# Expert weights fetched as 4 MB transfers instead of pairs of 2 MB ones

## The reference

```python
logits = h @ w_router + b_router;  top 4 of 32;  gate = softmax(top 4)
for each expert e, on the tokens that chose it:
    gu = xe @ w_gu[e] + b_gu[e]            # w_gu[e]: 1024 x 2048, 8 MB
    gt, up = split(gu);  gt = min(gt, 7);  up = clip(up, -7, 7)
    act = gt * sigmoid(1.702 * gt) * (up + 1)
    out = act @ w_dn[e] + b_dn[e]          # w_dn[e]: 1024 x 1024, 4 MB
y[token] += gate * out
```

## Time and profile before

| | |
|---|---|
| median of 3 runs | 1346.04 us (1345.9 to 1346.96) |
| the profiled execution | 1352.6 us, span 1350.5 us, mean granted TensorE clock 0.986 |
| PE busy | 1261.7 us, 93% of the span |
| DVE, ACT, POOL busy | 606.1, 207.5, 153.7 us |
| read from HBM | 472.06 MB, 353 GB/s over the span |
| chain that ended last | PE 74%, DMA 23%, DVE 2% |

### The profile page before, as it was taken

One profiled execution on the slowest core, in us unless ns is written; L12 is line 12 of the kernel. 1 busy time (PEld: TensorE's weight loads), 2 busy tenths in 40 slices (PEclk: granted clock), 3 DMA queues, 4 the chain that ended last, 5 costly groups with the idle time before them and its releaser, 6 DMA issues.

```text
span 1350.5 us, 18280 instructions
## 1 busy us (share of the span) xinstructions
PE 1261.7 (93%) x7708; PEld 524.7 (39%) x7708; DVE 606.1 (45%) x1013; ACT 207.5 (15%) x305; POOL 153.7 (11%) x177
## 2 busy tenths in 40 slices
PE   7999999999999989999999999999997878787885
PEld 5756766666553222233323332333322222222221
DVE  2898322311345563434434344535444444343445
ACT  4111433210311010001000000101000111000002
POOL 2110100000012120101111111102111121111000
PEclk9999999999989999999999999999999999999898
DMA  9714716464669999999999999999999999999993
GB/s 330 261 63 135 226 63 146 167 249 161 248 261 410 424 424 426 420 428 424 423 425 394 424 407 424 423 425 420 426 421 424 424 423 424 421 424 423 422 425 141
DMA packets 91229, 466.74 MB, mean 346 GB/s; under 512 B 41952, under 2 KB 44540, under 8 KB 66263
## 3 DMA queue, kind: packets, MB, share of 16 engines
q1 hardware_dynamic: 83489, 456.74, 83.3%
q0 software_dynamic: 6240, 5.37, 1.2%
q10 hardware_dynamic: 1374, 2.76, 0.6%
HBM read 472.06 MB, written 4.26 MB: 353 GB/s over the span
## 4 chain that ended last, share of the span: by engine, by line
PE 74%; DMA 23%; DVE 2%; issue 1%; SPq 0%; ACT 0%; DVEq 0%
PE PS L1757 26%; PE PS L1379 16%; PE PS L1787 14%; DMA ring<-in_w_gu 8%; DMA arena<-in_w_gu 8%; PE PS L1819 6%; DMA ring<-in_w_dn 5%; PE PS L1559 4%; DMA arena<-in_w_dn 3%; PE PS L1603 3%; PE PS L1415 2%; PE PS L1319 1%; PE PS L1646 1%; PE PS L1506 0%; DVE XX L1275 0%
## 5 line engine op out<-in xcount | busy, mean ns | idle before, releaser
L1757 PE MATMUL PS<-ring,arena 128*32 128x512 f32 x3408 | 388.8, 605 | 37.1 <-DMA ring<-in_w_gu 19.9
L1757 PEld LDWEIGHTS PS<-ring,arena 128*32 128x32 f32 x3408 | 108.4, 111 | 308.6 <-issue 300.4
L1379 PE MATMUL PS<-arena,ring 128*128 128x320 f32 x768 | 215.2, 436 | 0.1
L1787 PE MATMUL PS<-ring,arena 128*64 128x512 f32 x880 | 198.2, 600 | 14.3 <-DMA ring<-in_w_dn 14.3
L525 POOL DMA_INDIRECT arena<-h_rows,arena x120 | 129.9, 1083 | 710.6 <-DVE arena L1202 645.5
L1379 PEld LDWEIGHTS PS<-arena,ring 128*128 128x128 f32 x768 | 145.0, 191 | 59.6 <-issue 3.2
L1236 DVE TENSOR_TENSOR arena<-PS,XX 128x1024 f32<-128x1024 f32 x32 | 39.2, 1225 | 251.5 <-PE PS L1757 203.9
L795 ACT ACTIVATE arena<-arena 128x1024 f32<-128x1024 f32 x32 | 33.8, 1058 | 716.0 <-DVE arena L1241 716.0
L1757 PE MATMUL PS<-arena 128*32 128x512 f32 x1136 | 128.7, 594 | 8.6 <-DMA arena<-in_w_gu 6.5
L1787 PEld LDWEIGHTS PS<-ring,arena 128*64 128x64 f32 x880 | 62.2, 137 | 148.6 <-issue 148.5
L1172 DVE TENSOR_TENSOR XX<-PS,XX 128x1024 f32<-128x1024 f32 x32 | 39.2, 1224 | 155.5 <-PE PS L1819 155.5
(11 more groups left out here) (210 smaller groups left out, 754.3 us busy)
## 6 DMA issues: line engine op xcount, KB each, us to landing
ring<-in_w_gu SPq DMA_DIRECT2D x96, 2048.0 KB, 25.7
ring<-in_w_dn SPq DMA_DIRECT2D x46, 2048.0 KB, 24.4
arena<-in_w_gu SPq DMA_DIRECT2D x31, 2048.0 KB, 27.5
arena<-in_w_dn SPq DMA_DIRECT2D x17, 2048.0 KB, 30.4
ring<-in_w_in SPq DMA_DIRECT2D x11, 2048.0 KB, 11.1
ring<-in_w_mem_kv SPq DMA_DIRECT2D x2, 2048.0 KB, 20.9
ring<-in_cache_mem_k SPq DMA_DIRECT2D x32, 128.0 KB, 3.3
ring<-in_cache_mem_v SPq DMA_DIRECT2D x4, 1024.0 KB, 6.2
```

The source lines that it names most:

```text
L1379: last = mm(PS[:, j % 2, 0:T], w[:, k, m * P:(m + 1) * P], hT[:, k, :], start=k == 0, stop=k == KT - 1)
L1757: last = mm(PS[32 * q:32 * q + 32, 2 * i + b, :].rearrange("p (g n) -> p g n", g=2), xT[:, k, at:at + PART], w[:, :, q, :], start=k == 0, ...
L1787: last = mm(PS[64 * h:64 * h + 64, 4 + b, :], actT[:, 4 * c + j, b * BLK:(b + 1) * BLK], moe_ring(AT[(e, 4 + c)], 4)[:, j, h * 512:(h + 1) ...
```

## The change

From the chunk with turn 9 on (expert 2's first), each two neighbours in the stream, (e, 0) with (e, 1), (e, 2) with (e, 3), and (e, 4) with (e, 5), are fetched by one transfer of 4 MB, 32 KB a partition (`expert_pair`), under one semaphore. `PLACES` is turned so that the two lie in neighbouring places: turn 0 in place 7, turns 1 to 6 in places 0 to 5, turn 7 in place 6. The first eight chunks are still loaded one by one, into the places in the old order, so that each place now gets another chunk: (0, 0) goes to place 7 and is the sixth of them rather than the first. Before a pair SP waits until both places are free. PE's wait for either chunk of a pair is a wait for the whole transfer (`signalled`, `moe_loaded`, `moe_arrived`). Expert 31's two down chunks stay single. Nothing is changed in PE's, DVE's, ACT's or POOL's own instructions.

```diff
-PLACES = [(NMIX + i) % SLOTS for i in range(4)] + [SLOTS, SLOTS + 1] + [(NMIX + i) % SLOTS for i in (4, 5)]
+PLACES = [SLOTS + 1] + list(range(SLOTS)) + [SLOTS]
...
+def paired(i):
+    return i > RING and i % 2 == 1 and RINGED[i] < NCH - 2
...
+def signalled(i):
+    return PLACE[i - 1] if i and paired(i - 1) else PLACE[i]
...
 def moe_arrived(m, v):
-    s = moe_slot(m)
+    i = TURN[m]
+    s = signalled(i)
     mixer = -(-(NMIX - s) // SLOTS) if s < SLOTS else 0
-    turns = PLACE.count(s)
-    return 16 * (mixer + turns * v + PLACE[:TURN[m]].count(s) + 1)
+    own = [signalled(j) for j in range(len(RINGED)) if not (j and paired(j - 1))]
+    upto = [signalled(j) for j in range(i + 1) if not (j and paired(j - 1))]
+    return 16 * (mixer + own.count(s) * v + upto.count(s))
...
     def moe_loaded(m):
-        s = moe_slot(m)
+        s = signalled(TURN[m])
         return loaded[s] if s < SLOTS else low_in[s - SLOTS]
...
+        def expert_pair(m):
+            e, c = STREAM[m]
+            s = moe_slot(m)
+            rooms = ring[:, s:s + 2, :] if s < SLOTS else ring_low
+            if c < 4:
+                return sp.dma_start(rooms.rearrange("p s (k n) -> p (s k) n", k=2), wgu[e, :, 2 * c:2 * c + 4, :])
+            return sp.dma_start(rooms.rearrange("p s (k n) -> p (s k) n", k=4), wdn[e])
...
-        for i in range(RING):
-            m = RINGED[i]
-            if moe_slot(m) < SLOTS:
-                sp.wait_ge(*used_up[CHUNKS[NMIX - SLOTS + (i if i < 4 else i - 2)]])
+        for place in [(NMIX + i) % SLOTS for i in range(4)] + [SLOTS, SLOTS + 1] + [(NMIX + i) % SLOTS for i in (4, 5)]:
+            m = RINGED[PLACES.index(place)]
+            if place < SLOTS:
+                sp.wait_ge(*used_up[CHUNKS[next(n for n in range(NMIX - 1, -1, -1) if slot_of(n) == place)]])
...
+        def later(v, i):
+            if i and paired(i - 1):
+                return
+            m = RINGED[i]
+            if before_it(i) is not None:
+                free(v, RINGED[before_it(i)])
+            if paired(i):
+                free(v, RINGED[before_it(i + 1)])
+                expert_pair(m).then_inc(moe_loaded(m), 16)
+            else:
+                expert_chunk(m).then_inc(moe_loaded(m), 16)
+
         for i in range(RING, len(RINGED)):
-            free(0, RINGED[before_it(i)])
-            expert_chunk(RINGED[i]).then_inc(moe_loaded(RINGED[i]), 16)
+            later(0, i)
```

More of the change, by code:

```diff
@@ L439, in over_stream @@
                 bonus_part(i).then_inc(bonus_in, 16)
[L440 to L443, removed]
+            for i in range(len(RINGED)):
+                later(w, i)
             sp.wait_ge(main["dn_done"], NE * (w + 1))
```

## The result

The changed kernel takes 1349.41 us (median), before 1346.96 in the same comparison: ratio 1.0022, interval 1.0012 to 1.0032. A second build of it (E8) gave 1.0028 (1.0011 to 1.0044). By the medians it is slower by 2.5 us and the repeat by 4.5, by the ratios by 3.0 and 3.8; 4.2 were forecast.

A forecast was written before the change was run, and what follows sets the result against it. Bound: transfers up to 558 us, PE to 789, transfers to 1300.22, then PE and DVE. Late starts +7.0, larger pieces -1.0 and -3.5, clock +1.7 make +4.2: 1350.2 us, range 1348.7 to 1352.5.

The forecast's parts named there:

- First late start: Expert 5's down product near 558 us: (5, 4) now waits for (5, 5), +3.5 us kept until 789.
- fall of the clock: TensorE dropping to 1.2 GHz after longer waits: 1.7 us at each exposed place, one expected, bounds 0 and 3.4.
- The early stream: Transfers up to 558 us: larger pieces save 1.0 us over 15 pairs.
- the later first pair: Turns 9 and 10 now wait for both places, some 7 us later; taken as 0, between 0 and 2 us.
- The stream behind 789 us: Transfers from 789 to 1300 us: larger pieces save 3.5 us over 50 pairs.
- the forecast's fit: Main queue's 2 KB and 16 KB rates give 0.0373 ns a byte plus 8.2 ns a piece.
- rival 3: Both sides cancel: no clock fall on the path, 11 ns a piece; +1.1 us, 1347.1 us; chance 0.25.
- Second late start: Expert 31's gate-up near 1300 us: (31, 0) now waits for (31, 1), +3.5 us.
- The final transfers are not late for that: At the end: expert 31's down product begins only when DVE lets it, at 1326.21, so no added delay.
- Gathers: POOL's small pieces share engines with longer ones; landing of 8.0 us may near 16, cost taken as 0.
- Rival 1: Transfers clearly faster if a transfer's end or start costs the stream: 0.2 us a pair, 1341.7 us; chance 0.12.
- rival 2: Large pieces give nothing, only late starts and a clock fall remain: +8.7 us, 1354.7 us; chance 0.15.

The follow-up runs named there:

- E8: The full change built and run a second time, against the kernel before: 1351.61 us, ratio 1.0028.
- E1: Kernel before with its 2 MB transfers; only PE's wait widened to both chunks of a pair before starting the first: 1353.25 us, ratio 1.0041.
- E3: Changed kernel, but the pairs (31, 0) with (31, 1), (31, 2) with (31, 3), (30, 4) with (30, 5) stay 2 MB transfers: 1349.66 us, ratio 1.001.
- E6: Changed kernel with places reordered so three of four pairs aren't neighbours: still 4 MB transfers, those in 16 KB pieces: 1352.76 us, ratio 1.005.
- E5: Changed kernel, but only pairs from (7, 0) up to expert 27's down pair are 4 MB, chunks at both edges single: 1343.34 us, ratio 0.9972.
- E7: Kernel before, but each 2 MB chunk is fetched by two 1 MB transfers in 8 KB pieces, PE waiting for both: 1361.78 us, ratio 1.0102.
- E2: Changed kernel, but expert 5's two down chunks stay two 2 MB transfers: 1347.59 us, ratio 1.0002.
- E4: Changed kernel with expert 5's down chunks and the last three pairs all kept as single 2 MB transfers: 1345.74 us, ratio 0.9998.

## Why the prediction was right

The sign, the size (forecast 1350.2, measured 1349.41 us) and the mechanism held: two late starts, a faster stream that does not quite pay for them, and PE's regime in between that keeps what it gets. That the two times are only 0.8 us apart is partly luck: the growth was 2.5 to 3.0 us rather than 4.2, and the kernel before was itself 0.9 us slower in the comparison than the 1346.04 us from which I counted. The terms, in the trace's own time:

- First late start, +3.5 and at most one fall of the clock on the path: in E1, the full change and its repeat 5.5 to 5.6 us with the fall, in E3, which lacks it, 3.8. Right. The fall I had expected at one of the two places; it came at the first, 64 matmuls in 15.65 us.
- The early stream, -1.0: not there. With 340 MB left the stream is at -0.2, where E1, which has no larger pieces, is at -0.6, and expert 5's down pair starts 0.5 us later than (5, 5) did. What was mis-sized is the step "the later first pair", taken as 0 of a range of 0 to 2. SP issues this pair 7.8 us after turn 8 (390.57), where turn 9 followed after 0.4 us; SP's timeline of the changed kernel has it as the first of this group:

```profile
398.33 10.03 SPq L424 DMA_DIRECT2D ring<-in_w_gu  x2
```

The stream is 1.6 us late with 380 MB left in each kernel that starts with that pair (1.8 in E6), -0.1 in E1 and -0.3 in E5, which don't. The pairs that follow earn it back, and no more: 1.8 us from 380 to 340 MB, which is more than 10 pairs at 0.077 us give; E1 makes up 0.5 us there without them, and the rest stays open. I argued from when PE needs the pair; but the stream itself is on the path there, and its idle time counts, whoever is waiting.
- The stream behind 789 us, -3.5 for 50 pairs at 0.07 us: measured -4.0 from 240 to 20 MB left (52 pairs, 0.077 us each), in the repeat -3.8, in E1 -0.1. Right, with the cause shown by E6 and the slope between 2 KB and 16 KB pieces holding at 8 KB (E7) and at 32 KB: the forecast's fit gives 418 and 426 GB/s there, measured 417 and 427. One working beside it is not as it says: the 620 ns count only the 3554 pieces of 16 KB, by all 3997 packets of the earlier trace rows it would be 551 ns. The first fit, by which I forecast, does not need it; rival 3's 11 ns does.
- Second late start, +3.5: (31, 0) starts 0.2 us behind the time at which (31, 1) started before, and its own 3.5 us put (31, 1) at +3.7. E1 has 5.1 with a fall of the clock. Right. That the pair's start is at +0.2 while the stream is at +1.2 is 1.0 us more gain than the bytes show. A transfer counts as landed with the last of its 16 parts, the bytes are those of all. By the traces' landing records the last part of (31, 1) came 2.0 us after the main queue had 12.6 MB left in before (at 1300.22), 1.1 us after it in the changed kernel (at 1296.37); and PE then started after 0.1 us rather than 0.4. The size of the last transfer isn't the cause: in E5, where (31, 1) is a single chunk, the last part is 0.6 us behind, in E6, with 16 KB pieces, 0.8. Why the parts lie closer together in these runs stays open.
- "The final transfers are not late for that": wrong by 0.8 us. Expert 30's two down chunks now start together at 1317.04, and DVE's L1240 for expert 31 waits for their end, +3.8 at the end of the gate-up and +4.6 at the down product.
- Gathers, 0: their landing went from 8.0 to 11.3 us in the median (16.7 at most). It goes with the pieces: 10.7 to 12.0 us in all runs with 32 KB pieces throughout or in the middle, 8.4 in E6 with 16 KB in three of four pairs, 7.7 in E1. L1231 (L1202 before) still never waits for them:

```profile
DMA to landing us min/median/max: 6.8/11.3/16.7
L1231 DVE STREAM_TRANSPOSE arena<-arena 128x1024 f32<-128x1024 f32 x30 | 61.0, 2032 | 0.0
```

Sum as measured, in the order of time: 5.6 at expert 5's end, -0.4 to the stream's 5.2, -4.0 by the stream and -1.0 by the pair's arrival, +3.5 for the late start, +0.1 to the gate-up's end, +0.8 at expert 30's down product: 4.6. The sum as forecast, 4.2, is near it partly by luck: 1.4 too little up to expert 5's end and 0.8 at expert 30's down product, against 1.9 too little gain in between. The timed runs moved by less: by the ratios 3.0 us (1.6 to 4.3) and in the repeat 3.8 us (1.5 to 5.9); the first trace's 4.6 lies just above its interval, the second's 4.8 within. How often the clock falls on the path in unprofiled executions no trace shows, and this may be the rest.

Of the signs that I named, the waits came out only in part: from 1000 to 1300 us PE waits 24 times, 2.1 us on average, where it waited 39 times, 1.4 us on average; I had said 2.5 to 3 us and half as many. SP's issue near 789 comes 5.6 us later than before, counted from (1, 0), for the reasons above. None of the signs of being wrong is there.

Rival 1 (a transfer's own end costs) is out by E6, rival 2 (no gain) by the 427 GB/s. Of the Trainium skill's two sentences, that of "TensorE: Matmul & The Clock Gate" on bursts between waits was half right: from 1000 to 1300 us PEclk went from 0.97 to 0.95, with 9 falls for 24 waits (before 4 for 39), so more falls but not one behind each wait. That of "DMA: Bandwidth & Descriptors" on a fixed cost of each transfer, which the page fits for transfers that GpSimd issues, has no part in this stream, which SyncE issues and in which other transfers always stand in line behind 789 us: in E7 one transfer more a chunk cost 0.064 us, as much as its pieces.

## What to carry to other kernels

A coarser arrival costs nothing where the consumer is behind and nothing where it will wait again; it costs one unit's work where a wait is the last one before a dense stretch. Find these places by their last waits in the timeline and keep them fine, with several units of margin, since the exposure moves to a unit ahead when only one is mended. Judge larger pieces by the slope between two sizes that the trace already has, and compare profiled executions from a common event inside the stage, not from the start.

## What was not expected of the hardware

- Pieces of 32 KB a partition go on the same line as the smaller ones: all queues together 387 GB/s where the main queue has 2 KB pieces (28 to 46 us), and from 860 to 1000 us 417 at 8 KB, 423 at 16 KB, 427 at 32 KB, all with full engines.
- At expert 30's start PE stands still longer than its chunks need. By the landing records (30, 0) was there at 1264.38 in before, and PE began at 1269.33; in E2 the pair was there at 1264.55, and PE began at 1266.33. PE branches to other code at this point (`pe.If(most > WIN)`), and the instruction queue fetches 16 KB twice, at 1263.5 and 1263.8 us, but no run here shows that this is the cause.

```profile
1269.33 13.38 PE L1757 MATMUL PS<-ring,arena 128*32 128x512 f32 x96 [5.77 <-issue]
```

- TensorE's clock also falls near the start of the expert stage in some executions only: it is at 1.2 GHz for 10.2 us from 377.5 us on in the trace of before and for 6.8 us from 377 on in those of E2 and E4, and at full clock there in the other seven. (1, 0) starts 4.4 us later in before than in the changed kernel.
